# Four gated layers: another wait ahead of the next gate chunk, and tiles of its own for the last round's hidden product

## The reference

```
x = x + swiglu(rmsnorm(x, g), w13, w2)
# swiglu: hidden = silu(h @ w_gate) * (h @ w_up);  y = hidden @ w_down
```

## Time and profile before

| what | value |
|---|---|
| median of 3 runs | 2011.91 us |
| lowest and highest run | 2009.38 and 2022.34 us |
| the profiled execution's own time | 2022.98 us |
| its span in the trace | 2021.2 us |
| its mean granted TensorE clock | 0.984 of full speed |
| PE, DVE, ACT busy | 1922.5, 1377.1, 923.5 us |

### The profile page before, as it was taken

How to read it: one execution, slowest core, us unless ns; L and a number is a source line. 1 busy time by engine, 2 the same in 40 slices (tenths; PEclk the granted TensorE clock), 3 DMA queues, 4 the chain that set the end, 5 groups by cost and what they waited for, 6 DMA issues and landing times.

```text
span 2021.2 us, 32542 instructions
## 1 busy us (share of the span) xinstructions
PE 1922.5 (95%) x13424; PEld 1748.6 (87%) x13424; DVE 1377.1 (68%) x1577; ACT 923.5 (46%) x990; POOL 46.2 (2%) x65
## 2 busy tenths in 40 slices
PE   6999988999999989999999999998988999999999
PEld 6998887777777779999989999996878999999998
DVE  4767975766677666766667655567997565675555
ACT  4544843655656554433345443335334333444332
POOL 0000000000000000001101000000000000000000
PEclk8999998999999999999999999999999999999999
DMA  7553341777677756655553375553314555554552
GB/s 219 180 168 99 105 159 69 269 288 290 249 282 287 283 178 166 206 167 187 192 182 126 105 224 189 187 171 121 105 63 147 186 188 188 177 184 161 196 196 104
DMA packets 243915, 366.03 MB, mean 181 GB/s; under 512 B 12566, under 2 KB 217961, under 8 KB 231401
## 3 DMA queue, kind: packets, MB, share of 16 engines
q1 hardware_dynamic: 243817, 364.64, 53.6%
HBM read 363.57 MB, written 1.05 MB: 180 GB/s over the span
## 4 chain that ended last, share of the span: by engine, by line
PE 59%; DVE 11%; DMA 6%; ACT 5%; issue 3%; DVEq 0%; ACTq 0%; POOL 0%
PE proj L931 31%; PE acc L1265 11%; PE proj L950 6%; DMA raw<-in_w_exp_up_dram 6%; PE proj L1448 2%; DVE ring_lo L3110 2%; DVE ring_lo L2425 2%; ACT ring_hi L2152 2%; ACT second_hi L2152 1%; PE acc L1418 1%; ACT ring_hi L1864 1%; DVE second_lo L3110 1%; PE acc L1524 1%; PE acc L1278 1%; PE proj L1716 1%
## 5 line engine op out<-in xcount | busy, mean ns | idle before, releaser
L2425 DVE TENSOR_TENSOR ring_lo<-raw,ring_hi 128x2048 fp32r<-128x2048 f32 x242 | 560.0, 2317 | 215.3 <-ACT ring_hi L1864 214.1
L1864 ACT ACTIVATE ring_hi<-raw 128x2048 fp32r<-128x2048 f32 x242 | 462.3, 1914 | 446.7 <-PE proj L931 225.5
L931 PE MATMUL proj<-h_hi,ring_hi 128*128 128x256 f32 x1424 | 410.7, 288 | 13.9 <-DVE ring_lo L2425 9.8
L931 PE MATMUL proj<-h_lo,ring_hi 128*128 128x256 f32 x1424 | 398.9, 280 | 0.0
L931 PE MATMUL proj<-h_hi,ring_lo 128*128 128x256 f32 x1424 | 398.7, 280 | 0.0
L931 PE MATMUL proj<-g_hi,ring_hi 128*128 128x256 f32 x1088 | 304.6, 280 | 5.3 <-DVE hid L2958 4.1
L931 PE MATMUL proj<-g_lo,ring_hi 128*128 128x256 f32 x1088 | 303.3, 279 | 0.0
L931 PE MATMUL proj<-g_hi,ring_lo 128*128 128x256 f32 x1088 | 303.1, 279 | 0.0
L931 PEld LDWEIGHTS proj<-h_hi,ring_hi 128*128 128x128 f32 x1424 | 270.1, 190 | 26.3 <-issue 14.2
L931 PEld LDWEIGHTS proj<-h_lo,ring_hi 128*128 128x128 f32 x1424 | 270.8, 190 | 4.1 <-issue 3.2
L931 PEld LDWEIGHTS proj<-h_hi,ring_lo 128*128 128x128 f32 x1424 | 271.6, 191 | 0.0
(11 more groups left out here) (441 smaller groups left out, 3415.7 us busy)
## 6 DMA issues: line engine op xcount, KB each, us to landing
raw<-in_f_w_dram SPq DMA_DIRECT2D x132, 1024.0 KB, 5.0
raw<-in_w_exp_gate_dram SPq DMA_DIRECT2D x32, 1024.0 KB, 4.8
raw<-in_w_exp_up_dram SPq DMA_DIRECT2D x32, 1024.0 KB, 5.0
raw<-in_w_exp_down_dram SPq DMA_DIRECT2D x32, 1024.0 KB, 4.9
raw<-in_w_in_dram SPq DMA_DIRECT2D x29, 1024.0 KB, 5.3
raw<-in_a_w_in_dram SPq DMA_DIRECT2D x24, 1024.0 KB, 5.1
raw<-in_b_w_qkv_dram SPq DMA_DIRECT2D x12, 1024.0 KB, 5.1
raw<-in_c_w_in_dram SPq DMA_DIRECT2D x12, 1024.0 KB, 5.1
```

Of the source, the lines that this page charges most:

```text
L931: last = pe.matmul(bank[:, a, :], w[:, k, a * P:(a + 1) * P], h[:, k, :], start=(k == 0 and w is hi and h is h_h and (a == 0 or not first) ...
L1864: act.activation(w_hi[n.slot][:, :], raw[n.slot][:, :], ACT.Copy).then_inc(hi_ready, 1)
L2425: dve.tensor_tensor(w_lo[n.slot][:, :], raw[n.slot][:, :], w_hi[n.slot][:, :].bitcast(f32), SUB)\
```

## The change

- PE waits for `gate_scaled` instead of `banks_read` ahead of the next gate chunk. The wait for `banks_read` is moved behind it, ahead of the next up chunk.
- Two new tiles, `end_hi` and `end_lo`, are placed in the work area. In the last round (i = 9) DVE's split writes these, at once behind the product: ahead of the `part` of the up chunk, and without the wait for `chunk_used` of the down chunk. `down_last` reads them instead of `hid_hi` and `hid_lo`.
- So that the last round is written out in all four layers, `mlp_peel` gets the entry `"ffn2": 1`.

```diff
 def mlp_peel(name):
-    return {"ffn0": 1, "ffn1": 2, "ffn3": 1}.get(name, 0)
+    return {"ffn0": 1, "ffn1": 2, "ffn2": 1, "ffn3": 1}.get(name, 0)
...
+        end_hi = at("end_hi", [P, 2, SEQ], 8 * KB, f32r)
+        end_lo = at("end_lo", [P, 2, SEQ], 10 * KB, f32r)
...
                     for k in range(2):
-                        for h, w in ((hid_hi, hi), (hid_hi, lo), (hid_lo, hi)):
+                        for h, w in ((end_hi, hi), (end_hi, lo), (end_lo, hi)):
...
                     wait_parts(Chunk(c, g))
-                    pe.wait_ge(banks_read, i + (base + 1))
+                    pe.wait_ge(gate_scaled, i + (base + 1))
                     product_f(Chunk(c, g), operand, False)
                     wait_parts(Chunk(c + 1, g))
+                    pe.wait_ge(banks_read, i + (base + 1))
                     product_f(Chunk(c + 1, g), operand, False)
...
-                def split(i):
-                    link(dve.tensor_copy(hid_hi[:, :, :], hid[:, :, :]))
-                    dve.tensor_tensor(hid_lo[:, :, :], hid[:, :, :], hid_hi[:, :, :].bitcast(f32), SUB).then_inc(hid_ready, 1)
+                def split(i, hi=hid_hi, lo=hid_lo):
+                    link(dve.tensor_copy(hi[:, :, :], hid[:, :, :]))
+                    dve.tensor_tensor(lo[:, :, :], hid[:, :, :], hi[:, :, :].bitcast(f32), SUB).then_inc(hid_ready, 1)
...
                     product(i + 1, Chunk(c + 1, g))
-                    part(Chunk(c + 1, g))
-                    dve.wait_ge(chunk_used, Chunk(c + 2, g).used)
-                    split(i + 1)
+                    if isinstance(i, int) and i == rounds - 1:
+                        split(i + 1, end_hi, end_lo)
+                        part(Chunk(c + 1, g))
+                    else:
+                        part(Chunk(c + 1, g))
+                        dve.wait_ge(chunk_used, Chunk(c + 2, g).used)
+                        split(i + 1)
                     part(Chunk(c + 2, g))
```

More of the change, by code:

```diff
@@ L1276, in down_last @@
                     for k in range(2):
-                        for h, w in ((hid_hi, hi), (hid_hi, lo), (hid_lo, hi)):
+                        for h, w in ((end_hi, hi), (end_hi, lo), (end_lo, hi)):
                             last = pe.matmul(acc[:, 2 * t + m, :], h[:, k, t * P:(t + 1) * P],
                                              w[:, k, m * HALF:(m + 1) * HALF], start=False,
-                                             stop=(k == 1 and h is hid_lo), skip_group_check=True)
+                                             stop=(k == 1 and h is end_lo), skip_group_check=True)
                     last.then_inc(chunk_used if q == 3 else acc_done, 1)
```

## The result

The changed kernel takes 2006.77 us, the median of 14 runs (2004.81 to 2013.35). The kernel before, run 14 times beside it, takes 2019.03 us (2009.38 to 2030.27). The ratio is 0.9948, with a 95% interval of 0.993 to 0.9965: by it the change is 10.5 us faster (7 to 14), which is within 1%; the two medians lie 12.3 us apart. The forecast was 1997.3 us with a range of 1989 to 2006; the result lies 0.8 us above the range. The three runs of before that the forecast started from had a median of 2011.91 us, 7.1 us under the median of fourteen.

What follows compares the result with a forecast made beforehand. PE was taken to bound the kernel, with only its waits removable. Finer wait 8.2, clock 5.0 and ffn3's end 1.4 summed to 14.6 us, taken off the runs' median: 1997.3 us, range 1989 to 2006.

Steps and rivals of the forecast that it cites:

- The finer wait: At gate 1 of each layer, PE's whole idle of 2.06 us goes; 8.2 us for four layers.
- the new wait ahead of up 1: banks_read's wait moves ahead of up 1; covered by the 5.5 us gate product, it costs nothing.
- it costs 1.7 us of PE's work, three times 5.0 us: Clock falls behind the gate waits of ffn0, ffn2 and ffn3 cost 1.7 us each; 5.0 us regained, bounds 0 to 6.7.
- the mixed rows: Clock windows behind the gate waits: 0.79 in ffn0, ffn2 and ffn3, 1.00 in ffn1; 5.0 us would vary by run.
- the rival by which the clock is not given back: Clock falls only come at another place: 9.6 us gained, 2002.3 us; chance 0.18.
- The early split: At layer ends, down_last's wait is replaced by one at the turn; only ffn3 keeps its gain, 1.4 us.
- What the split delays: The up chunk's low part comes 1.1 us later but is used some 10 us later; costed at nothing.
- the written-out round: ffn2's last round written out instead of looped: at most 0.1 us either way, taken as 0.
- The loop's rival: ffn3's moved loop waits for instructions, up to 8 times 3.6 us, 28.8 us: 2026.1 us; chance 0.04.
- leaves about 2: ffn1's first rounds: gate 2's low part, ready at 1208.5, keeps about 2 us of margin after the 2.05 us gain.
- I take the full 14.6 off the median: The whole 14.6 us gain is subtracted from the runs' median, though the profiled execution lay 11 us above it: 1997.3 us.
- behind the shorter waits (1.3 to 1.7 us) the clock was never lowered: At layer ends, waits of 1.3 to 1.7 us brought no clock fall; used to expect none without the gate idle.

Runs made afterwards that it cites:

- the early split alone: Changed kernel with the old wait (banks_read ahead of the next gate chunk): 2018.71 us, ratio 1.0003 to the kernel before.
- the moved low part with the old split: Kernel before with the last down 9 chunk's low part behind all quarters' adds, ffn2's last round written out: 2033.01 us, ratio 1.0075.
- before again: The kernel before, unchanged, profiled a second time to count the clock's falls: one execution, 2019.41 us.
- the finer wait alone: Kernel before with gate_scaled ahead of the next gate chunk and banks_read ahead of the next up chunk, no early split: 2003.86 us, ratio 0.9931.
- the longer wait: Kernel before with gate 1 of each layer waiting for the split (hid_ready) too: 2042.78 us, ratio 1.0115.
- the low part between the adds: Changed kernel with the last down 9 chunk's low part behind the first two quarters' adds: 2002.12 us, ratio 0.9906 to before; again 2002.07 us, 0.9919.
- the changed kernel again: The changed kernel, unchanged, timed a second time: 2007.88 us, ratio 0.9938 to the kernel before.
- the kernel with the split in ffn3 alone: Changed kernel with the early split only in ffn3 and ffn2's last round back in its loop: 2009.03 us, ratio 0.9939 to before.
- the low part moved behind the adds: Changed kernel with the last down 9 chunk's low part behind all quarters' adds and the turned norm's low parts: 2014.83 us, ratio 0.9984 to before.

## Why the prediction was right in part, and which steps failed

**The finer wait: right, in place and in size.** The 8.2 us of idle went, nothing late took their place, and the new wait ahead of up 1 never appeared. Its worth without the clock is read from the nine gate waits (in the four profiles with the old wait) behind which the clock did not fall. In four of them the first two stretches between gate scalings are 12.69 and 16.49 us, in four they are 12.88 or 12.89 and 16.80, in one 12.88 and 16.91. Both kinds stand in the second profile of before, in ffn1 and in ffn2:

```profile
1190.55 0.69 DVE L2949 TENSOR_TENSOR gate_in<-proj,inv_b 128x512 f32<-128x512 f32 x1
1203.24 0.69 DVE L2949 TENSOR_TENSOR gate_in<-proj,inv_b 128x512 f32<-128x512 f32 x1 [2.39 <-PE proj L931]
...
1553.37 0.69 DVE L2949 TENSOR_TENSOR gate_in<-proj,inv_b 128x512 f32<-128x512 f32 x1
1566.26 0.69 DVE L2949 TENSOR_TENSOR gate_in<-proj,inv_b 128x512 f32<-128x512 f32 x1 [2.59 <-PE proj L931]
```

With the finer wait they are 10.59 and 16.81. So a layer gains 1.78 us against the first kind and 2.3 against the others, 2.07 on average, and four layers gain 8.3 us. The two kinds differ by the pace of PE's matmuls. At the start of a layer PE's matmuls of a gate or up product run at one pace, 0.35 us for three (866.73 to 867.08), and later at a quicker one; here both ends of fifteen of them in round 2:

```profile
890.81 0.28 PE L933 MATMUL proj<-g_hi,ring_lo 128*128 128x256 f32 x1
...
892.51 0.28 PE L933 MATMUL proj<-g_hi,ring_lo 128*128 128x256 f32 x1
```

1.70 / 15 = 0.113 us each against 0.117, both at a granted clock of 1.00. With the old wait the quicker pace began behind the idle in 11 of 16 starts, all seven with a fall among them. In the other five, and with the finer wait, it begins at the earliest with the first down chunk. Two products of 48 matmuls at 0.004 us more are 0.4 us, near the 0.5 by which the two kinds differ. Why it is so is open.

**The clock: right mechanism, a term of twice its size.** The step that failed is "it costs 1.7 us of PE's work, three times 5.0 us". With a fall the two stretches are 14.30 and 16.49 us, 1.61 us more than 12.69 and 16.49, as said, and 1.3 us more than the mean of the nine without a fall. But over the four profiled executions with the old wait (before, the early split alone, the moved low part with the old split, before again) the falls came in ffn0 4 times of 4, in ffn1 0, in ffn2 1, in ffn3 2: 7 in 16 waits, not 3 in 4. In the seven profiles with the finer wait none came there. The term is 4 x 7/16 x 1.3 = 2.3 us, and by counts so small it is rough. The prediction had the mixed rows and said that the 5.0 would be an average that varies; it should then have priced the falls below what one execution showed. The rival by which the clock is not given back is not borne out: the finer wait alone gains more than it allows, and the longer wait shows that this wait brings the falls. It may still hold for a part. At ffn1's end the clock fell in three of the four profiles that have the finer wait and no moved low part, and in one of the five with the old wait. The runs are too few to tell this from chance.

**The early split: right about the turns; ffn1's end was missed.** ffn3's `down_last` starts 1.40 us earlier, and from the last gate scaling to the end of the kernel it takes 19.54 us instead of 21.20, 1.66 less. ffn0's and ffn2's ends gained 0.18 and 0.09 us. The working of the cause held as well: the adds stand behind the low part and not behind PE, as the low part between the adds shows. What was not foreseen is that the clock could fall at ffn1's end. Behind the idle of 1.65 us it fell in 2 of 6 profiles, and the next stage's first product came only 0.05 us later, since PE waits for the adds anyway. Behind the one of 2.65 us it fell in 2 of 3, and there it does cost. The last gate scaling of ffn1 and the next stage's first product, in the changed kernel (no fall) and in the changed kernel again, with its window behind the wait:

```profile
1350.31 0.69 DVE L2952 TENSOR_TENSOR gate_in<-proj,inv_b 128x512 f32<-128x512 f32 x1
1370.09 0.37 PE L933 MATMUL proj<-h_hi,ring_hi 128*128 128x256 f32 x1
```

```profile
1350.67 0.69 DVE L2952 TENSOR_TENSOR gate_in<-proj,inv_b 128x512 f32<-128x512 f32 x1
1371.29 0.37 PE L933 MATMUL proj<-h_hi,ring_hi 128*128 128x256 f32 x1
```

```profile
1366.00:1374.00 8.00, 7.53 (x44) 6.34 (x45) 4.74 (x11) 4.54 (x14) 0.00 (x0) 0.79 0.31 98
```

1370.09 - 1350.31 = 19.78 us became 20.62, and behind the norm the delay is 1.1 us. At 2 times in 3 that is about 0.7 us lost, a rough figure.

**What the split delays, and the written-out round: costed at nothing, rightly**, as the kernel with the split in ffn3 alone shows. The loop's rival did not come true: ffn3's rounds are 16.40 us. One margin was thinner than "leaves about 2". In the profiled execution after, ACT waited 5.6 us for the load of a chunk at ffn1's start. The low part for gate 2 was done at 1206.21 us, and PE began gate 2 at 1206.35 after 0.11 us of idle. In the other six profiles with the finer wait PE did not wait there.

**The sum against both scales.** Resized: 8.3 + 2.3 + 1.66 + 0.27 - 0.7 = 11.8 us, against 10.5 measured (7 to 14). In the profiled pair, where before happened to have three falls behind its gate waits and after none, the gain was 15.0 us, near the forecast's 14.6. That nearness is luck: the single pair flattered the forecast.

**The start.** The step that put the number outside its range is "I take the full 14.6 off the median": the median of three runs. With the median of 14 the same sum gives 2019.03 - 14.6 = 2004.4 us, inside the range; with the resized terms as well it gives 2019.03 - 11.8 = 2007.2, against 2006.77 measured. The range allowed 3 to 4 us for the runs' spread although the three runs lay 13 us apart; and it left the side of a smaller gain at the rival's 2002.3 plus that. A median of three such runs is itself uncertain by more, here by 7 us. The text under the chances has a slip besides: it counts its last rival as slower by over 1%, but the 2026.1 us that it gives is 0.7% slower.

## What to carry to other kernels

When a wait of the bounding engine is for the reader of one buffer and the next product writes another, wait for what that product needs; check that the wait, moved, is covered by the product. A wait at the end of a layer is worth only what the next one leaves: follow it to the instruction that the following stage cannot pass (here the adds behind a low part), and move that one; but see whose port the moved work blocks. Price a fall of the clock by how often it comes over several profiles, and take no number off a median of three.

## What the runs showed that was not expected

- How often the clock falls rises with the idle ahead of it, in these layers: behind at most 0.95 us never, behind 1.34 to 1.40 us in none of 17, behind 1.65 us at ffn1's end in 2 of 6, behind 2.05 us in 7 of 16, behind 2.6 us in 2 of 3, behind 5.55 us in 4 of 4. The length is not all: the waits of 2.05 us were followed by a fall in ffn0 each time and in ffn1 never. The prediction's "behind the shorter waits (1.3 to 1.7 us) the clock was never lowered" held for the one execution it looked at. A window behind a wait of 1.64 us, at the end of ffn1 (finer wait, split in ffn3 alone):

```profile
1361.00:1369.00 8.00, 7.52 (x28) 6.07 (x29) 7.04 (x12) 1.42 (x4) 0.00 (x0) 0.79 0.81 264
```

- PE has two paces at a full granted clock, 0.113 and 0.117 us for a matmul of a product. All of ffn1 ran at the slower one in the profiles of before and after (rounds of 16.82 us), at the quicker one in before again (16.40): 0.42 us in nine rounds, 3.8 us. The cause is open. The pace is one source of the spread between executions. The clock is another: over a whole profile the granted clock averaged from 0.990 (finer wait alone) to 0.981 (the low part moved behind the adds), so from 20 to 38 us of full clock are missing, idle time included.
- A GpSimd instruction on 2 columns takes 0.19 us, and 1.92 to 2.11 us when DVE's low parts run beside it.
